# Both halves of the normed activations moved 32 bytes along in on-chip memory, in a kernel of three transformer blocks on one core

## The reference, cut to what matters

```
h = modulate(rms_norm(x, g), shift, scale)            # 256 x 1024
x = x + 0.5 * gate * ((silu(h @ w_gate) * (h @ w_up)) @ w_down)   # 1024 -> 2816 -> 1024
```

## Time and profile before

| | |
|---|---|
| median of 3 runs | 1282.73 us (1281.85 to 1286.23) |
| span of the profiled execution | 1280.1 us, first to last instruction |
| its own time | not recorded apart from the span |
| TensorE matmul busy | 1258.1 us (98%) |
| VectorE busy | 1007.1 us (79%) |
| ScalarE busy | 601.9 us (47%) |
| mean granted TensorE clock | 0.996 |

### The profile page before, as it was taken

How to read it: one execution, slowest core, us unless ns; L and a number is a source line. 1 busy time by engine, 2 the same in 40 slices (tenths; PEclk the granted TensorE clock), 3 DMA queues, 4 the chain that set the end, 5 groups by cost and what they waited for, 6 DMA issues and landing times.

```text
span 1280.1 us, 26147 instructions
## 1 busy us (share of the span) xinstructions
PE 1258.1 (98%) x11088; PEld 1228.4 (96%) x11088; DVE 1007.1 (79%) x1652; ACT 601.9 (47%) x859; POOL 89.1 (7%) x159
## 2 busy tenths in 40 slices
PE   9999999999999999999999999999999999999997
PEld 7899999998999999999999989999999987999997
DVE  4899998876888667999988867899965957766665
ACT  4544335575433635433335665333344466633333
POOL 0111110000111040111110000000001000000000
PEclk9999999999999999999999999999999999999999
DMA  9999997441888653999994424545543423455551
GB/s 369 384 397 384 376 355 287 150 147 39 326 342 323 238 200 119 346 370 355 360 379 134 162 98 150 220 175 198 200 149 117 160 75 113 180 199 190 188 191 42
DMA packets 66101, 293.89 MB, mean 230 GB/s; under 512 B 7745, under 2 KB 8897, under 8 KB 51905
## 3 DMA queue, kind: packets, MB, share of 16 engines
q1 hardware_dynamic: 47552, 225.10, 48.1%
q0 software_dynamic: 18432, 67.12, 13.1%
HBM read 291.14 MB, written 1.05 MB: 228 GB/s over the span
## 4 chain that ended last, share of the span: by engine, by line
PE 87%; DVE 6%; ACT 2%; DMA 2%; SPq 2%; issue 1%; DVEq 0%; ACTq 0%
PE gu_bank L642 16%; PE gu_bank L644 15%; PE gu_bank L643 15%; PE y_bank L642 7%; PE y_bank L644 7%; PE y_bank L643 7%; PE t_bank L642 3%; PE t_bank L644 2%; PE t_bank L643 2%; DVE dn_lo L1816 2%; PE gu_bank L629 1%; DMA raw_gu<-ffn_gu 1%; PE gu_bank L694 1%; PE gu_bank L698 1%; PE gu_bank L695 1%; SPq L469 1%
## 5 line engine op out<-in xcount | busy, mean ns | idle before, releaser
L642 PE MATMUL gu_bank<-hT_hi,gu_hi 128*128 128x256 f32 x1668 | 461.5, 277 | 3.8 <-DVE hT_lo L1802 1.6
L643 PE MATMUL gu_bank<-hT_lo,gu_hi 128*128 128x256 f32 x1668 | 460.7, 276 | 0.0
L644 PE MATMUL gu_bank<-hT_hi,gu_lo 128*128 128x256 f32 x1668 | 460.7, 276 | 0.0
L642 PEld LDWEIGHTS gu_bank<-hT_hi,gu_hi 128*128 128x128 f32 x1668 | 313.1, 188 | 5.1 <-issue 3.4
L644 PEld LDWEIGHTS gu_bank<-hT_hi,gu_lo 128*128 128x128 f32 x1668 | 313.1, 188 | 0.0
L643 PEld LDWEIGHTS gu_bank<-hT_lo,gu_hi 128*128 128x128 f32 x1668 | 313.1, 188 | 0.0
L1821 DVE TENSOR_TENSOR gu_lo<-raw_gu,gu_hi 128x2048 fp32r<-128x2048 f32 x105 | 240.8, 2293 | 39.3 <-ACT gu_hi L1326 34.1
L1326 ACT ACTIVATE gu_hi<-raw_gu 128x2048 fp32r<-128x2048 f32 x100 | 191.1, 1911 | 40.0 <-DMA raw_gu<-ffn_gu 40.0
L1343 ACT ACTIVATE sg<-gu_bank 128x256 f32<-128x256 f32 x88 | 33.8, 385 | 354.2 <-PE gu_bank L644 354.2
L642 PE MATMUL y_bank<-act_hi,dn_hi 128*128 128x256 f32 x660 | 183.2, 278 | 0.0
L643 PE MATMUL y_bank<-act_lo,dn_hi 128*128 128x256 f32 x660 | 182.3, 276 | 0.0
(11 more groups left out here) (508 smaller groups left out, 2169.5 us busy)
## 6 DMA issues: line engine op xcount, KB each, us to landing
raw_gu<-ffn_gu SPq DMA_DIRECT2D x110, 1024.0 KB, 6.3
stage<-ada POOLq DMA_DIRECT2D x128, 512.0 KB, 7.7
raw_dn<-ffn_dn SPq DMA_DIRECT2D x110, 512.0 KB, 3.7
ring<-mix_w SPq DMA_DIRECT2D x72, 512.0 KB, 3.6
stage<-ada SPq DMA_DIRECT2D x8, 512.0 KB, 14.1
pro<-ada SPq DMA_DIRECT2D x6, 512.0 KB, 12.9
x<-x_in SPq DMA_DIRECT2D x1, 1024.0 KB, 5.8
ring<-ada SPq DMA_DIRECT2D x2, 512.0 KB, 17.4
```

The source lines that it names most:

```text
L642: pe.matmul(to, a[0], b[0], start=start, stop=False)
L643: pe.matmul(to, a[0], b[1], start=False, stop=False)
L644: return pe.matmul(to, a[1], b[0], start=False, stop=stop)
```

## The change

Two filler tensors are added that nothing reads or writes. The first, 8 floats or 32 bytes, lies ahead of `hT_hi`; the second, 24 floats or 96 bytes, behind `hT_lo`. `hT_hi` and `hT_lo` then start at remainder 32 instead of 0. Everything after them moves by 32 + 96 = 128 bytes and keeps its remainder. No instruction is added, removed or reordered.

```diff
         hT = sb(ctx, "hT", [P, KC, S])
+        sb(ctx, "halves_gap", [P, 8])
         hT_hi = sb(ctx, "hT_hi", [P, KC, S], F32R)
         hT_lo = sb(ctx, "hT_lo", [P, KC, S], F32R)
+        sb(ctx, "halves_end", [P, 24])
         raw_gu = sb(ctx, "raw_gu", [P, 2, 2 * KC * P])
```

## The result

The changed kernel takes 1316.48 us (1315.5 to 1317.24, four runs) against 1284.48 us before (1281.85 to 1286.47, four runs on the same chip): a ratio of 1.0254, 95% interval 1.0241 to 1.0268. It is slower by 32 us. The profiled execution has a span of 1314.0 us, 33.9 more than before's, at a granted clock of 0.995: the 2.4 GHz level, as before. Of the four executions with both activations at 48, further down, one showed a clock of 0.846 and took 1404 us, and the ratio given there is taken without it.

What follows compares the result with a forecast made beforehand. The prediction took TensorE, busy 98% of the span, as the bound. Terms of 18.8, 3.6 and 1.8 us made 24.2 us; with span 1280.1 and 2.6 around it, 1306.9, say 1306 us, range 1268 to 1313.

Steps and rivals of the forecast that it cites:

- the long rhythm: Likeliest case: products with hT take the slower steady pitch, 117.5 ns instead of 113.3; 1306 us, chance 0.38.
- the hand-over to the down products: At some 105 returns between gate-and-up and down products, four steps lose 4.2 ns each: 1.8 us.
- Relative, not absolute: Claim that TensorE's pitch depends on how moving operand and next weights lie to each other in address; no separate size.
- The pitch of the gate and up products: In the feed-forward bodies, 4466 products with hT each take 4.2 ns longer: 18.8 us.
- The rest: Mixers, prologue and body ends: 1730 products, half counted at each pitch, so 865 lose 4.2 ns: 3.6 us.
- the short rhythm: The faster of TensorE's two steady pitches before the change, 113.3 ns per product, seen in the feed-forward bodies.
- Nothing happens: Rival: the moved buffer falls into the same two rhythms; 1282.7 us within 3 us, chance 0.28.
- Faster: Rival: heads and mixers, or all products, run shorter; chance 0.27, of which 0.13 to 1277 and 0.14 down to 1252.
- Much slower: Rival: delays of 8.4 ns a product, 50 us more, 1333 us; chance 0.07.
- The rule that spoke against: Trainium skill: independent read ports and 16-byte memory lines, so addresses change nothing and time stays at 1282.7 us.

Runs made afterwards that it cites:

- both activations at 48: Kernel before with the halves of hT and the hidden activations all put 48 bytes behind their tensors' starts: 1315.19 us, ratio 1.0246.
- everything moved along: Changed kernel without its second filler, so the halves start at 32 and all behind them moves by 32 too: 1282.47 us, ratio 0.9997.
- streams alone: Separate kernels with only TensorE working, 96 products per stream; place is the moving operand's start by 256 bytes, weights at 64: 113.5 ns at 0, 119.9 at 64.
- the halves at 64: Changed kernel with fillers of 16 and 16 floats, so the halves of hT start at 64: 1318.76 us, ratio 1.0275.
- at 96: Changed kernel with fillers of 24 and 8 floats, so the halves of hT start at 96: 1303.49 us, ratio 1.0154.
- behind by 128: Kernel before with one 128-byte filler behind hT_lo, moving everything behind the halves by 128: 1298.05 us, ratio 1.0104.
- 32 alone: Changed kernel with the second filler at 56 floats, so tensors behind the halves move by 256 bytes: 1322.59 us, ratio 1.0301.
- both halves at 48 in one tensor: Kernel before with hT_hi and hT_lo in one shared tensor, both at 48 by 256 bytes: 1295.39 us, ratio 1.0099.
- the alternation by itself: TensorE alone, 48 products at one place then 24 at another, four times: 48 at 32 and 24 at 0 had 118.2 and 114.8 ns.
- all weights at 144: Kernel before with gate, up, down and mixers' weights at 144 by 256 bytes, all moving operands at 0: 1334.06 us, ratio 1.0406.

## Why the prediction was right, and where it was not

Right: slower, by the pitch of the products alone. The direction had 0.45, the case "the long rhythm" 0.38. Wrong: the size. 1306 was forecast with 1268 to 1313, and 1316.5 lies 3.5 us over the range. All three terms of the sum came out too small, and the one that failed by most is the hand-over to the down products: 1.8 us forecast, 6.2 measured.

*Where the time goes.* As said: TensorE's share as before, other engines' durations as before. The windows answered to the test that the prediction named, 1345 matmuls expected and 1330 found where 1379 was "nothing" and more was "faster". Nothing else was needed for the 33.9 us.

*Relative, not absolute.* The prediction put it to how the two streams lie in address; everything moved along costs nothing (0.9997), and streams alone at the places 64 and 160 lose their delay when the weights' address stands still (119.9 to 113.4 and 113.5 ns). This much of the mechanism is shown, for multiples of 32; at odd multiples of 16 equal distances gave 120.0 and 113.3. The prediction's own case for it was weaker than it says. ScalarE was not as busy after the clears as in the head (2.87 against 6.94 us in 9), and the clears part products with `hT` from products with `act`, whose places differ by 128 in the unit of 256. "Where they lie" calls all distances 64; that holds by 128 only.

*The pitch of the gate and up products, 4466 x 4.2 = 18.8 us.* Mis-sized. The long rhythm was taken because it was the only other one seen. The products did not fall into it: they have a pitch of their own, 118.3 ns on the mean of 84 steps of the bodies, 5.0 more than before. 4466 x 5.0 = 22.3 us, 3.5 more than forecast. The range of other pitches (116.8 to 120.0 at the next distances) shows that the value could not be had from the trace of before; that the long rhythm's 117.5 came within 1 ns of it is luck.

*The rest, 865 x 4.2 = 3.6 us.* 28.2 - 22.3 = 5.9 us, 2.3 more. The mixers' products were put at the pitch of the gate and up products, but they lie at place 160, and before the change those that go to the y and t banks were mostly in the short rhythm, not half in each: 114.1 to 119.8 ns over 529 steps. (The count of 6576 also takes in some 120 value products of another form, 512 columns wide, which had no term of their own.) The heads, 471 steps by chunk, went from 117.8 to 118.4, as good as unmoved, as forecast.

*The hand-over to the down products, 1.8 us.* The step that failed. Down products keep their distance, and the forecast let them lose four steps per visit, as after the clears. They lost 6.2 us: 45 of their 89 steps of 24 run in the long rhythm, the others in the short one; 45 x 23 x 4.5 ns is 4.7 us. Before the change it was 1 of 87. Where hardly a visit stayed long the priced part was about right: 2620 steps went from 113.55 to 114.05 ns with the halves at 64 and to 114.36 at 96, 1.3 and 2.1 us. That rhythm is not set by the distance of their own operands: at the same distance it was 0 of 89 with the halves at 64, 2 of 89 at 96, 35 of 88 behind by 128, 36 of 89 with 32 alone, and 86 of 88 with both halves at 48 in one tensor. Something outside these products decides, and the stream that comes before is the likeliest, but the alternation by itself did not show it. The prediction had the fact in hand (two rhythms over the same addresses, and "stays in one until something shifts it") and priced only the shift, not the staying.

Together 3.5 + 2.3 + 4.4 = 10.2 us over the 24.2, so 34.4 us, where the span grew by 33.9.

*A step nobody priced.* That moving everything behind by 128 bytes changes nothing was taken for granted with the remainders of 128. It costs some 13 us alone, 1.0104. The rows gave no evidence for a period of 128.

*The rivals.* "Nothing happens" fell with the first count. "Faster" fell too: no place tried gave the gate and up products less than 113.3 ns, and the best of the kernels, everything along, is level with the one before. "Much slower", 8.4 ns a product and 1333 us, is not what the change did, but all weights at 144, which slows the down products as well, came to 1334.06.

*The rule that spoke against.* The pitch of a 256-column product moved with the relation of its two operands, from 113.3 to 120.0 ns in the kernels and up to 123 alone. By the Trainium skill, TensorE: Matmul & The Clock Gate, section Step-by-step: what each phase is for, the two read ports are independent and loading takes nothing from the running product; by this rule all would be equal, and the runs disagree. The lines of 16 bytes that the Trainium skill gives in SBUF — State Buffer, section Door 1, would let 32 bytes be neutral; the pitches at the places 0 and 32, 113.5 and 118.3 ns, disagree. Of the four places off the multiples of 16 two have the longest pitches of all (122.8) and one has 117.2, so these runs neither show nor exclude lines of that size.

*What stays open.* Why the short and the long rhythm both exist at places 0 and 128, and what decides between them: why the down steps take turns in the change, keep one rhythm through a whole body in two other kernels, and why the bodies of the kernel before run short at place 128. Whether the unit is 256 bytes or more. Why 144 for all weights gave 120.0 where its distance had 113.8 alone. Why the alternation by itself did not show the long rhythm in the second stream. These were run, not explained. Which part of an access delays the other cannot be seen in a trace of starts and ends.

## What to carry to other kernels

Where TensorE is busy 98% of the time with products that each have a weight load of their own, look at the pitch from start to start, not at busy shares, and take the placement of the moving and the loaded operands as something that costs: here two fillers, 32 and 96 bytes, cost 2.5% and one of 128 bytes 1%, and no placement tried was better than the one there was. Try placements as a set, by their remainder of 256 at least, with the kernel's own alternation of streams, since a sweep of one stream finds the bad places but not which rhythm a mixed sequence settles in. And when one trace shows two rhythms over equal addresses, price the case that a stream stays in the other one.

## What was not expected of the hardware

- A product of 128 x 128 weights and 256 float32r columns at the full clock has a pitch between 113.3 and 123 ns, by where its operands start: with weights at 64, 113.5 at place 0, 118.3 at 32, 119.9 at 64. At some places it has either of two, and a stream can keep one of them: 113.3 or 117.8.
- The relation repeats neither by 128 bytes (places 48 and 176 have 117.1 and 113.8 ns) nor, at odd multiples of 16, by distance alone (at 144, 120.0 or 113.3 in two kernels).
- Moving the low halves alone slows the whole sequence of three products as much as moving both: 118.9 ns against 118.3.
- With the same column streamed again and again the pitch is 112.0 ns, still 5.3 over the 106.7 of 256 columns at 2.4 GHz.
- With the same weights address again and again the two slowest places, 64 and 160, fall from 119.9 to 113.4 and 113.5 ns.
